# Attention with V as the stationary operand: split values and split, turned probabilities in half sequences, outputs scaled at the end, and half of the preparation on GpSimd

## The chip, the cores and the metric

The kernel runs on one NeuronCore of a Trainium2 chip. The metric is device time of one execution in microseconds (us), as the median of several runs. The page of the profile and every trace row come from one profiled execution. Engines are called as the profile calls them: PE is TensorE (PEld its weight loads), DVE is VectorE, ACT is ScalarE, POOL is GpSimd, SP is SyncE, which here issues most of the transfers.

## What is computed

Two sequences of 512 tokens (plus 16 meta tokens each, so 528 positions per sequence) go through a two-layer encoder: an attention mixer, a feed-forward block, a state-space mixer, a second feed-forward block. The change touches the attention mixer alone. Cut to what matters:

```python
SEQ, N_META = 512, 16                 # two sequences of 528 positions
MLA_HEADS, QK_HEAD_DIM, V_HEAD_DIM = 16, 96, 64

def mla_mixer(u, w_in, q_norm, kv_norm, w_q_up, w_kv_up, q_head_norm, k_head_norm, w_out):
    c_q, c_kv, k_rope = jnp.split(u @ w_in, [384, 640], axis=-1)
    q = (rmsnorm(c_q, q_norm) @ w_q_up).reshape(b, L, 16, 96)
    kv = (rmsnorm(c_kv, kv_norm) @ w_kv_up).reshape(b, L, 16, 128)
    k_nope, v = jnp.split(kv, [64], axis=-1)
    k = jnp.concatenate([k_nope, broadcast(k_rope)], axis=-1)
    q, k = apply_rope(rmsnorm(q, q_head_norm), pos), apply_rope(rmsnorm(k, k_head_norm), pos)
    s = einsum('bqhd,bkhd->bhqk', q, k) / sqrt(96)
    p = softmax(s, axis=-1)
    o = einsum('bhqk,bkhd->bqhd', p, v)
    return o.reshape(b, L, 1024) @ w_out
```

Everything is float32. Most products are made from split operands: a value is written as high + low, both in a rounded type that TensorE multiplies in one pass (`F32R`, fp32r in the rows), and three products (high by high, high by low, low by high) are summed.

## The kernel before

The work is written out by hand as one instruction stream for each engine; semaphores alone order them against each other. Activations lie transposed, features on partitions and the 2 x 528 positions along the free dimension. The program goes through: first norms and the two low-rank projections, attention, the output projection (units `U_OUT`), feed-forward, state-space layer, feed-forward, final norm.

**The attention stage** is a loop over 16 heads `j` and, inside each, 10 turns `n`; turn number `t = 10 j + n`. A turn handles one block of 106 queries (`CW`; five blocks cover a sequence, the last overlaps the one ahead of it by two) against all 528 keys of its sequence. `nxt = j + 1` is the head that is prepared meanwhile. Every engine runs the same double loop, with its own list of what it does in turn `n`:

- PE, `scores(t)` L1489 on: six matmuls of 264 columns (three products of split Q and K by two halves of the keys) into the two banks from `A_SCORE`. There is one such pair of banks, so they wait for the exponentials of turn `t - 1` (`p_full`); only in the last head two pairs alternate (`score_bank`).
- PE, `turn_probs(t - 1)` L1507 on: five transposes that turn the probabilities of the turn before, keys onto partitions (rows of L1513).
- PE, `outputs(t - 2)` L1516 on: five float32 matmuls with the turned probabilities `PT` (106 x 106) stationary and 64 columns of `V` moving (L1528; a float32 matmul leaves two records each).
- PE, then preparation for the next head: `project_q` in turns 0 to 3, `query_norms` (4 and 5), `turn_outputs` of the pair before last (L1479 on), `project_k` (turns 6, 7) and `key_norms` (8, 9) in every even head up to 12, `project_v` (6 to 9) in heads 3, 7 and 11.
- DVE: `take_k` ahead of the turn's maximum where there are keys, then `maximum(t)` (a reduction over the 528 scores L3007, then its scaling L3010), `take_turned(t - 1)` (copy of three transposed blocks, L3018), `invert(t - 1)` (reciprocal of the row sum), then the rest: `scale_keys`, `turn_queries`, `low_q`, `low_k`, `low_weights`, and the small chains `key_factors` (turns 0 and 1 of odd heads) and `query_factors`.
- ACT: `take_q`, `take_k`, `take_turned(t - 1)` (the two other blocks, L2306), `exponentials_of(t)` (L2318, with the sums of the rows), `evict(t - 2)` (outputs times the reciprocal, 106 x 64), then the high halves of Q, K and of weights.
- POOL does nothing from before the first head until the last one, where it splits outputs and weights for the output projection.
- SP loads the weights, saves the key factors of a pair to DRAM and loads them back broadcast over partitions (`save_factors`, `load_factors`).

A pair is two heads (64 + 64 output rows). The outputs of a head lie with queries on partitions in `O`; `turn_outputs` transposes them and ACT copies them to `H` (`take_outputs_of`).

PE does its list strictly in order, so an instruction that waits holds back the next turn's scores. One wait of this kind matters below: bank `A_STAT` takes one set of sums at a time,

```python
def key_norms(p, half):
    pe.wait_ge(k_squared, NSEQ * p + half + 1)
    if half == 0:
        wait_stats("k", p)      # until what stood in A_STAT ahead of it was taken
```

and what stands there ahead of the key sums is the query sums, which the first instruction of `query_factors(nxt, 0)` on DVE takes.

## Time and profile before

| | |
|---|---|
| median of 3 runs | 3041.29 us |
| lowest, highest | 3038.35, 3042.91 us |
| span of the profiled execution | 3038.7 us |
| of that: PE busy | 2967.0 us (98%) |
| DVE, POOL, ACT busy | 1924.1 (63%), 1527.5 (50%), 1176.6 us (39%) |
| granted TensorE clock, mean | 0.992 |

The span runs from the first to the last instruction of the profiled execution; no separate whole time of that execution is given, and the median lies 2.6 us above its span. Busy shares are means over stages that differ; the attention stage with its 160 turns is some 515 us of the span. Matmul records are pipelined and overlap each other, so the distance between two starts on PE tells more than one record's length.

### The profile page before, as it was taken

How to read it: one execution, taken by the hardware profiler on the slowest of the kernel's cores; microseconds unless marked ns; L12 is line 12 of the kernel's file. 1: busy time of each engine (PE TensorE's matmuls, PEld its weight loads, DVE VectorE, ACT ScalarE, POOL GpSimd, SP SyncE). 2: the span in 40 equal slices, each digit the busy share in tenths (PEclk: the TensorE clock that was granted, in tenths of full speed). 3: DMA queues.
4: the chain of work that ended last, by engine and by line, in shares of the span. 5: the costliest groups of instructions: out<-in, count | busy, mean ns of one | idle time of the engine just before them, and what ended most of it. 6: DMA issues, size and time to landing. Idle time of an engine off the chain costs nothing.

```text
span 3038.7 us, 50018 instructions
## 1 busy us (share of the span) xinstructions
PE 2967.0 (98%) x19166; PEld 2684.5 (88%) x19166; DVE 1924.1 (63%) x2960; ACT 1176.6 (39%) x2027; POOL 1527.5 (50%) x997
## 2 busy tenths in 40 slices
PE   8999999999999999999999999999999999999998
PEld 8999999999999999999999988677777788888776
DVE  6677777755534445777788851677778934445666
ACT  4465666641333334553111122232323533334552
POOL 4100000043777777765444444467674577777774
PEclk9999999999999999999999999999999999999998
DMA  3000100021223334442233423333333232235442
GB/s 128 26 30 27 37 26 16 16 100 49 72 95 99 103 100 163 140 144 71 87 117 94 138 90 118 116 119 101 123 94 118 67 107 102 99 103 171 149 130 90
DMA packets 195934, 286.73 MB, mean 94 GB/s; under 512 B 14709, under 2 KB 105077, under 8 KB 195701
## 3 DMA queue, kind: packets, MB, share of 16 engines
q1 hardware_dynamic: 156096, 236.23, 23.8%
q10 hardware_dynamic: 39605, 47.34, 4.7%
q8 instruction: 154, 2.52, 0.3%
q14 instruction: 79, 0.65, 0.1%
HBM read 208.64 MB, written 74.86 MB: 93 GB/s over the span
## 4 chain that ended last, share of the span: by engine, by line
PE 80%; DVE 7%; POOL 5%; issue 4%; DMA 2%; ACT 1%; SPq 1%; DVEq 0%; ACTq 0%; POOLq 0%
PE PS L1272 72%; PE PS L1528 4%; PE PS L1513 2%; DMA Wraw<-in_w 1%; POOL Wlo L1108 1%; POOL Wlo L1168 1%; PE PS L1872 1%; POOL SQ L1213 1%; SPq L911 0%; DVE GD L3627 0%; POOL RMS L1178 0%; POOL Wraw L1126 0%; POOL Wraw L1124 0%; DVE MX L3007 0%; PE PS L2024 0%
## 5 line engine op out<-in xcount | busy, mean ns | idle before, releaser
L1272 PE MATMUL PS<-Uhi,Whi 128*128 128x352 f32 (+2 forms) x2028 | 512.4, 328 | 16.5 <-DVE Ulo L2799 13.8
L1272 PE MATMUL PS<-Uhi,Wlo 128*128 128x352 f32 (+2 forms) x2028 | 507.3, 326 | 0.0
L1272 PE MATMUL PS<-Ulo,Whi 128*128 128x352 f32 (+2 forms) x2028 | 507.0, 326 | 0.0
L1108 POOL TENSOR_TENSOR Wlo<-Wraw,Whi 128x512 fp32r<-128x512 f32 x242 | 329.8, 1366 | 130.4 <-ACT Whi L2442 127.1
L1272 PEld LDWEIGHTS PS<-Uhi,Whi 128*128 128x128 f32 x2028 | 340.9, 189 | 39.4 <-issue 15.9
L1067 POOL TENSOR_TENSOR Whi<-Wraw,const 128x1024 fp32r<-128x1024 f32 x64 | 159.1, 2486 | 418.4 <-PE PS L1272 403.4
L1272 PEld LDWEIGHTS PS<-Ulo,Whi 128*128 128x128 f32 x2028 | 343.5, 189 | 20.3
L1272 PEld LDWEIGHTS PS<-Uhi,Wlo 128*128 128x128 f32 x2028 | 343.4, 189 | 19.5
L2442 ACT ACTIVATE Whi<-Wraw 128x512 fp32r<-128x512 f32 x242 | 151.3, 629 | 330.7 <-POOL Wraw L1126 133.3
L1156 POOL TENSOR_TENSOR Olo<-H,Ohi 128x1056 fp32r<-128x1056 f32 x5 | 12.1, 2444 | 521.8 <-ACT Ohi L2345 521.8
L1272 PE MATMUL PS<-T,Whi 128*128 128x264 f32 (+1 forms) x1328 | 219.1, 288 | 2.1 <-DVE H L3311 1.9
L1272 PEld LDWEIGHTS PS<-T,Whi 128*128 128x128 f32 x1328 | 186.5, 188 | 3.0 <-DVE H L3311 2.4
L3007 DVE TENSOR_REDUCE MX<-PS 106x1 f32<-106x528 f32 x160 | 113.1, 707 | 113.1 <-PE PS L1272 112.4
L3498 DVE SCALAR_TENSOR_TENSOR YC<-XC,cols,YC 128x1052 f32<-128x1052 f32 (+1 forms) x96 | 180.8, 1883 | 3.4
L1070 POOL TENSOR_TENSOR Wlo<-Wraw,Whi 128x1024 fp32r<-128x1024 f32 x64 | 177.0, 2765 | 5.0
L1528 PE MATMUL PS<-V,PT 106*106 106x64 f32 x1600 | 170.0, 254 | 0.5 <-ACT O L2329 0.5
L1528 PEld LDWEIGHTS PS<-V,PT 106*106 106x106 f32 x1600 | 161.8, 173 | 0.6 <-issue 0.6
L2318 ACT ACTIVATE PR<-PS,MX,TOK 106x528 f32<-106x528 f32 x160 | 127.0, 794 | 47.3 <-DVE MX L3010 46.9
L1272 PE MATMUL PS<-T,Wlo 128*128 128x264 f32 (+1 forms) x664 | 135.3, 287 | 0.0
L1272 PE MATMUL PS<-Uhi,OPS 128*128 128x264 f32 (+1 forms) x552 | 126.0, 321 | 1.3 <-DVE H L3311 0.7
L3311 DVE TENSOR_TENSOR H<-H,PS 128x528 f32<-128x528 f32 x140 | 98.1, 700 | 45.3 <-PE PS L1272 43.5
L3330 DVE TENSOR_TENSOR H<-H,PS 128x512 f32<-128x512 f32 x140 | 94.1, 683 | 49.9 <-PE PS L1272 49.9
(431 smaller groups left out, 7114.4 us busy)
## 6 DMA issues: line engine op xcount, KB each, us to landing
Wraw<-in_w SPq DMA_DIRECT2D x192, 256.0 KB, 3.0
Wraw<-in_w SPq DMA_DIRECT2D x91, 512.0 KB, 3.7
Wraw<-in_w SPq DMA_DIRECT2D x168, 128.0 KB, 2.7
xt<-XTT ACTq DMA_DIRECT2D x20, 640.0 KB, 5.7
opd<-HID SPq DMA_DIRECT2D x40, 264.0 KB, 3.4
T<-opd SPq DMA_DIRECT2D x18, 528.0 KB, 4.3
Ulo<-opd SPq DMA_DIRECT2D x17, 528.0 KB, 4.8
Ulo<-opd SPq DMA_DIRECT2D x17, 512.0 KB, 5.5
```

The lines of the kernel that those rows point to most:

```text
L1067: pool.tensor_tensor(Whi[s][:], Wraw[s][:], ones.unsqueeze(1).broadcast_to([P, BLK, P]), ALU.mult)\
L1070: pool.tensor_tensor(Wlo[s][:], Wraw[s][:], Whi[s][:].bitcast(F32), ALU.subtract)\
L1108: pool.tensor_tensor(f.oplo[j % SLOTS], FIRST_S2 if (p, k) == (0, 6) else f.factors[k], f.ophi[j % SLOTS].bitcast(F32), ALU.subtract).then ...
L1272: ins = pe.matmul(out, lhsT, rhs, start=start, stop=stop, skip_group_check=True)
L1513: ins = pe.transpose(PS[0:CW, A_TURN + b // TURN_DVE, b % TURN_DVE * CW:(b % TURN_DVE + 1) * CW], PR[t % 2][:, key_start(b):key_start(b) + ...
L1528: ins = pe.matmul(PS[0:CW, A_OUT, 0:VD], PT[t % 2][:, b, :], V[x // 4 % 2][:, n // KB * KB + b, x // 2 % 2, x % 2 * VD:(x % 2 + 1) * VD], ...
L2318: act.activation(PR[t % 2][:].rearrange("p (h n) -> p h n", h=2), PS[0:CW, score_bank(t):score_bank(t) + 2, 0:QHALF], ACT.Exp, bias=MX[:, ...
L2442: act.activation(f.ophi[j % SLOTS], FIRST_S2 if (p, k) == (0, 6) else f.factors[k], ACT.Copy)\
L3007: step(vec.tensor_reduce(MX[:, t % RING:t % RING + 1], PS[0:CW, score_bank(t):score_bank(t) + 2, 0:QHALF], AX_XY, ALU.max))
L3311: vec.tensor_tensor(h, h, f.down_bank(k, x), ALU.add).then_inc(f.added.sem, 1)
L3330: vec.tensor_tensor(h, h, f.down_bank(k, x), ALU.add).then_inc(f.added.sem, 1)
L3498: ins = vec.scalar_tensor_tensor(y_[:, :, to], x[:, :, of], taps[:, tap:tap + 1], y_[:, :, to], ALU.mult, ALU.add)
```

## The change

Everything lies in the attention stage. `outputs` now works on a half sequence: for head `x`, sequence `s` and half `h`, the stationary operand is a block of values `VH` whose 128 columns are the head's 64 values in high and in low form side by side, and 264 columns of turned probabilities move, first their high part (`PTH`), then their low part (`PTLa`, `PTLb`). The 64 output rows from the high and the 64 from the low values are added afterwards, by ACT (`other_half`) and DVE (`add_outputs`), straight into `H`. There are 4 such steps in a head in place of 10, in the turns that `PV_TURNS` names (11 is turn 1 of the next head). The row sums are kept in `TOK`, inverted once per pair, saved to DRAM and loaded back spread over partitions, and POOL multiplies `H` by them; the last pair is scaled on DVE out of PSUM. `turn_queries`, `scale_keys`, `low_q`, `low_k` and `low_weights`, and the high half of K for odd heads, move to POOL.

```diff
+PV_TURNS = {4: (0, 0), 6: (0, 1), 9: (1, 0), 11: (1, 1)}
...
-        def outputs(t):
...
-            for b in range(KB):
-                ins = pe.matmul(PS[0:CW, A_OUT, 0:VD], PT[t % 2][:, b, :],
-                                V[x // 4 % 2][:, n // KB * KB + b, x // 2 % 2, x % 2 * VD:(x % 2 + 1) * VD],
-                                start=(b == 0), stop=(b == KB - 1), skip_group_check=True)
+        def outputs(x, s, h):
+
+            pe.wait_ge(pt_high, 2 * last_block(x, s, h) + 2)
+            pe.wait_ge(pt_low, 2 * last_block(x, s, h) + 2)
+            pe.wait_ge(v_lo, x + 1)
+            if (x, s, h) != (0, 0, 0):
+                pe.wait_ge(o_evicted, half_number(x, s, h))
+            of = slice(h * QHALF, (h + 1) * QHALF)
             for b in range(KB):
+                low = PTL[b // TURN_FIRST][:, b % TURN_FIRST, of]
+                for i, probs in enumerate((PTH[:, b, of], low)):
+                    ins = mm(PS[:, A_OUT, 0:QHALF], VH[x % 2][:, s * KB + b, :], probs,
+                             start=(b == 0 and i == 0), stop=(b == KB - 1 and i == 1))
...
# ACT, one turn
                 if t >= 1:
-                    take_turned(t - 1)
-                if t >= 0:
-                    exponentials_of(t)
-                if t >= 2:
-                    evict(t - 2)
+                    high_turned(t - 1)
+                exponentials_of(t)
+                if half_at_turn(t, 1):
+                    other_half(*half_at_turn(t, 1))
+                if j and j % 4 == 0 and n == 1:
+                    high_values(j)
                 if nxt < HEADS:
-                    if n == 5:
+                    if n == 3 and nxt % 4:
+                        high_values(nxt)
+                    if n == 6:
                         high_q(nxt)
-                    if n == (1 if nxt % 2 else 6):
+                    if n == 7 and nxt % 2 == 0:
                         high_k(nxt)
...
# DVE, one turn
-                if t >= 0:
-                    maximum(t)
+                maximum(t)
                 if t >= 1:
-                    take_turned(t - 1)
-                    invert(t - 1)
+                    low_turned(t - 1)
+                if half_at_turn(t, 1):
+                    add_outputs(*half_at_turn(t, 1))
+                if j and j % 2 == 0 and n == 1:
+                    invert(j // 2 - 1)
                 if nxt < HEADS:
                     if nxt % 2 == 0 and n < 2:
                         key_factors(nxt // 2, n)
-                    if n == (0 if nxt % 2 else 5):
-                        scale_keys(nxt)
-                    if n == 4:
-                        turn_queries(nxt)
-                    if n == (7 if nxt % 2 else 6):
-                        low_q(nxt)
-                    if n == (2 if nxt % 2 else 7):
-                        low_k(nxt)
-                    if n in ((6, 9) if nxt % 2 else (8, 9)):
+                    if n in (8, 9):
                         query_factors(nxt, n == 9)
...
+        def low_turned(t):
...
+            for b, (k0, k1) in enumerate(((0, TURN_FIRST), (TURN_FIRST, KB))):
+                vec.wait_ge(pt_high, 2 * t + b + 1)
+                vec.tensor_tensor(PTL[b][:, :, at],
+                                  PS[0:CW, A_TURN + b, 0:(k1 - k0) * CW].rearrange("p (b q) -> p b q", q=CW)[:, :, dup:],
+                                  PTH[:, k0:k1, at].bitcast(F32), ALU.subtract).then_inc(pt_low, 1)
...
+        def add_outputs(x, s, h):
+
+            own, n = slice(x % 2 * VD, (x % 2 + 1) * VD), half_number(x, s, h)
+            vec.wait_ge(ob_made, n + 1)
...
# POOL, new: one head
+            if nxt % 2:
+                scale_keys(nxt)
+            if j and j % 4 == 0:
+                low_values(j)
+            if nxt % 2:
+                high_k(nxt)
+                low_k(nxt)
+            if nxt % 4:
+                low_values(nxt)
+            if j % 2 and split_unit(j) is not None:
+                low_weights(j)
+            if j >= 4 and j % 2 == 0:
+                scale_outputs(j // 2 - 2)
+            turn_queries(nxt)
+            if j % 2 == 0 and split_unit(j) is not None:
+                low_weights(j)
+            if nxt % 2 == 0:
+                scale_keys(nxt)
+            low_q(nxt)
+            if nxt % 2 == 0:
+                low_k(nxt)
...
# SP, new: per pair
+        def load_sums(p):
+
+            sp.wait_ge(sums_out, 16 * (p + 1))
+            if p:
+                sp.wait_ge(o_scaled, p)
```

Two places of the order matter below. The first is PE in turn 4 of an even head. Before (rows are engine instructions in program order, `KHI,QHI` are scores, `const,PR` the transposes, `V,PT` the outputs, `const,SQ` the query norms):

```order
L1272 MATMUL PS<-KHI,QHI 106x264 [waits p_full]
L1272 MATMUL PS<-KHI,QHI 106x264
L1272 MATMUL PS<-KLO,QHI 106x264 x2
L1272 MATMUL PS<-KHI,QLO 106x264 x2
L1513 MATMUL PS<-const,PR 106x106 [waits pt_scalar,pt_vector,p_full]
L1513 MATMUL PS<-const,PR 106x106 x4
L1528 MATMUL PS<-V,PT 106x64 [waits o_evicted,pt_scalar,pt_vector]
L1528 MATMUL PS<-V,PT 106x64 x4
L1272 MATMUL PS<-const,SQ 106x1 [waits stats_taken,q_squared]
L1272 MATMUL PS<-const,SQ 106x1 x4
```

The same turn in the changed kernel, from the transposes on (`out_pool` is `v_lo` there):

```order
L1666 MATMUL PS<-const,PR 106x106 [waits pt_low,p_full]
L1666 MATMUL PS<-const,PR 106x106 x2
L1666 MATMUL PS<-const,PR 106x106 [waits pt_low]
L1666 MATMUL PS<-const,PR 106x106
L1417 MATMUL PS<-PTH,VH 128x264 [waits out_pool,o_evicted,pt_low,pt_high]
L1417 MATMUL PS<-PTLa,VH 128x264
L1417 MATMUL PS<-PTH,VH 128x264
L1417 MATMUL PS<-PTLa,VH 128x264
```

Five short output matmuls of each turn became ten of 264 columns in turns 1, 4, 6 and 9 (six more like these follow the last row), and none in turns 0, 2, 3, 5, 7 and 8. The second place is DVE in the even heads with a next pair of keys: before, in turn 6, the query factors begin right behind the reciprocal:

```order
L3007 TENSOR_REDUCE MX<-PS 106x1 [waits sc_full]
L3010 TENSOR_SCALAR MX<-MX,TOK 106x1 [waits vec_steps]
L3018 COPY PT<-PS 106x318 [waits ov_full,pt_full]
L3026 RECIPROCAL SINV<-SSUM 106x1 [waits o_evicted,p_full]
L2940 TENSOR_TENSOR TOK<-PS,TOK 106x10 [waits stats_full]
```

Now they begin in turn 8, behind `take_k` (L3054) and the two subtractions of the low probabilities:

```order
L3165 TENSOR_TENSOR H<-PS,OB 64x264 [waits h_half]
L3054 TENSOR_SCALAR KR<-PS,cols 64x528 [waits k_scaled,k_squared]
L3139 TENSOR_REDUCE PS<-PS 106x1 [waits sc_full]
L3144 TENSOR_SCALAR MX<-PS,TOK 106x1 [waits p_full,vec_steps]
L3154 TENSOR_TENSOR PTLa<-PS,PTH 106x3x106 [waits pt_high]
L3154 TENSOR_TENSOR PTLb<-PS,PTH 106x2x106 [waits pt_high]
L3089 TENSOR_TENSOR TOK<-PS,TOK 106x10 [waits stats_full]
```

The last row is the one that frees bank `A_STAT` for the key norms (`h_half` is `ob_made` here); it moved by two turns, into the same turn as the first `key_norms` of PE.

## Rows read from the trace of the kernel before

**Rows 1.** Busy time by engine from the first maximum to head 15's.

```profile
core 0: us, PE busy (x) PEld busy (x) DVE busy (x) ACT busy (x) POOL busy (x), PEclk, DMA share, GB/s
121.90:614.40 492.50, 479.43 (x4532) 474.80 (x4533) 358.56 (x1025) 308.38 (x753) 0.00 (x0) 1.00 0.07 24
```

**Rows 2.** Timeline of turn 7 of head 5 (start us, us, engine, line, op).

```profile
307.81 0.49 PE L1272 MATMUL PS<-KHI,QHI 128*106 128x264 f32 x2
...
308.63 0.62 PE L1513 MATMUL PS<-const,PR 106*106 106x106 f32 x5
308.83 0.71 DVE L3007 TENSOR_REDUCE MX<-PS 106x1 f32<-106x528 f32 x1 [0.37 <-PE PS L1272]
...
309.08 1.06 PE L1528 MATMUL PS<-V,PT 106*106 106x64 f32 x10
...
309.82 0.79 ACT L2318 ACTIVATE PR<-PS,MX,TOK 106x528 f32<-106x528 f32 x1
...
309.98 0.62 PE L1485 MATMUL PS<-const,O 106*128 106x106 f32 x5
...
310.76 0.48 PE L1272 MATMUL PS<-KHI,QHI 128*106 128x264 f32 x2 [0.15 <-ACT PR L2318]
```

**Rows 3.** Timeline, turns 6 to 8 of head 2, which projects keys.

```profile
206.29 0.49 PE L1272 MATMUL PS<-Chi,Whi 128*128 128x264 f32 x2
...
206.50 0.15 DVE L2940 TENSOR_TENSOR TOK<-PS,TOK 106x10 f32<-106x10 f32 x1
...
207.71 0.17 DVE L2828 SCALAR_TENSOR_TENSOR TOK<-TOK 106x10 f32<-106x10 f32 x1
...
207.85 0.41 PE L1272 MATMUL PS<-KHI,QHI 128*106 128x264 f32 x2
...
208.05 0.61 ACT L2256 ACTIVATE SS<-PS 128x528 f32<-128x528 f32 x1 [0.81 <-PE PS L1272]
...
208.75 0.77 DVE L2905 TENSOR_SCALAR KR<-PS,cols 64x528 f32<-64x528 f32 x1 [0.87 <-ACT SS L2256]
...
209.56 0.71 DVE L3007 TENSOR_REDUCE MX<-PS 106x1 f32<-106x528 f32 x1
...
211.48 0.49 PE L1272 MATMUL PS<-KHI,QHI 128*106 128x264 f32 x2
```

**Rows 4.** Timeline of DVE: first maximum of heads 0, 4, 5, 6, 7, 8, 15.

```profile
121.88 0.69 DVE L3007 TENSOR_REDUCE MX<-PS 106x1 f32<-106x528 f32 x1
...
254.18 0.69 DVE L3007 TENSOR_REDUCE MX<-PS 106x1 f32<-106x528 f32 x1
...
286.76 0.71 DVE L3007 TENSOR_REDUCE MX<-PS 106x1 f32<-106x528 f32 x1 [0.34 <-PE PS L1272]
...
317.73 0.71 DVE L3007 TENSOR_REDUCE MX<-PS 106x1 f32<-106x528 f32 x1 [0.23 <-PE PS L1272]
...
351.58 0.71 DVE L3007 TENSOR_REDUCE MX<-PS 106x1 f32<-106x528 f32 x1 [0.33 <-PE PS L1272]
...
386.65 0.69 DVE L3007 TENSOR_REDUCE MX<-PS 106x1 f32<-106x528 f32 x1
...
614.42 0.71 DVE L3007 TENSOR_REDUCE MX<-PS 106x1 f32<-106x528 f32 x1 [0.23 <-PE PS L1272]
```

**Rows 5.** Groups by line and shape, whole span: prices for new and moved instructions.

```profile
L3647 DVE TENSOR_TENSOR SQ<-PS,EXPC 128x512 f32<-128x512 f32 x32 | 22.0, 686 | 3.2 <-PE PS L1272 3.0
...
L2336 ACT ACTIVATE H<-PS 128x424 f32<-128x424 f32 x16 | 8.3, 522 | 2.4 <-PE PS L1485 2.4
...
L1070 POOL TENSOR_TENSOR Wlo<-Wraw,Whi 128x1024 fp32r<-128x1024 f32 x64 | 177.0, 2765 | 5.0
...
L1156 POOL TENSOR_TENSOR Olo<-H,Ohi 128x1056 fp32r<-128x1056 f32 x5 | 12.1, 2444 | 521.8 <-ACT Ohi L2345 521.8
...
L2794 DVE TENSOR_TENSOR SS<-SS,SQ 128x1056 f32<-128x1056 f32 x9 | 15.5, 1722 | 0.6
```

**Rows 6.** Stretches around the two falls of the granted clock, columns as above.

```profile
111.00:114.40 3.40, 3.40 (x35) 3.40 (x35) 3.33 (x5) 2.17 (x2) 0.00 (x0) 1.00 0.51 160
114.50:117.90 3.40, 3.40 (x18) 3.40 (x17) 2.18 (x10) 0.00 (x0) 0.00 (x0) 0.50 0.00 0
...
636.70:640.10 3.40, 2.68 (x25) 2.43 (x25) 0.67 (x3) 1.00 (x4) 2.37 (x2) 1.00 0.18 74
```

More of the change, by code:

```diff
@@ L371, in key_start @@
     return w // KB * L + min(w % KB * CW, L - CW)
-def turned_pair(j):
-    return j // 2 - 1 if j % 4 == 2 or j % 4 == 1 and j > 1 else None
 def prep_orders():
@@ L389, in prep_orders @@
             stats.append(("t", nxt // 2))
+        elif j:
+            stats.append(("s", j // 2 - 1))
         stats.append(("q", nxt))
-        if turned_pair(j) is not None:
-            prep += [("o", turned_pair(j), s) for s in both]
         if nxt % 4 == 0:
@@ L1583, in _ @@
                         query_norms(nxt, n - 4)
-                    o = 4 if nxt % 2 else 6
-                    if turned_pair(j) is not None and o <= n < o + 2:
-                        turn_outputs(turned_pair(j), n - o)
                     if nxt % 4 == 0 and n >= 6:
@@ L2385, in _ @@
         t = HEADS * PER_HEAD
-        take_turned(t - 1)
-        evict(t - 2)
-        evict(t - 1)
-        take_outputs_of(PAIRS - 1, 1)
+        high_turned(t - 1)
+        for h in range(2):
+            other_half(HEADS - 1, 1, h)
         high_out(PAIRS - 1)
```

387 lines of the change are left out of this document (231 added, 156 removed).

## The prediction

> **What bounds the kernel now.** I read the busy shares first, then the attention stage alone, then single turns. From the first maximum to that of head 15, 492.5 us pass, with PE busy for 479.4 of them, the clock at 1.00 and POOL at nothing [rows 1]. That looks like a stage bound by PE, but the timeline of one turn says otherwise. Scores start at 307.81, the maximum at 308.83 (1.02 later), the exponentials at 309.82 (2.01), the next scores at 310.76: 2.95 us, and that last start waited for ACT [rows 2]. There is one pair of score banks, so scores, maximum, its scaling, exponentials and scores again form a **loop of 2.95 us** that no saving on PE shortens. PE's own list takes longer than the loop in some turns only. Its pieces: scores and transposes 1.27 (307.81 to 309.08), outputs 0.90 (309.08 to 309.98) [rows 2], key projection 1.56 for 12 matmuls of 264 columns (206.29 to 207.85) [rows 3], so 0.13 for each. A turn with nothing else is 2.17 on PE and runs at 2.95; with a first query part (10 matmuls, 1.30) it is 3.47, with a second (8, 1.04) 3.2, with a set of norms (10 short records; at the outputs' 0.09 each, 0.90) 3.07.
>
> A third limit sits in the even heads that project keys. In their turn 7, ACT squares the keys from 208.05, DVE copies them from 208.75, and the maximum starts at 209.56, 1.71 after its scores at 207.85 instead of 1.02; the next scores follow at 211.48, 3.63 later [rows 3]. Turn 8 has the same piece.
>
> A head takes 32.6 us (254.18 to 286.76: keys), 31.0 (to 317.73: odd), 33.9 (to 351.58: keys and turned outputs) or 35.1 (to 386.65: values) [rows 4].
>
> **The change, part by part,** as what each turn costs over the loop of 2.95.
>
> Loop. The maximum goes through PSUM and scaling reads it there; copies and sums from PSUM and SBUF differ by little in price, so 0. ACT now puts two copies (318 and 212 columns; from 0.52 for 424 [rows 5], 0.44 and 0.35 are estimates) ahead of the exponentials where it had one. The transposes end about 1.45 into the turn, the first three about 1.28; the two copies can be through by 1.9, and the exponentials start at 2.01. Loop stays 2.95. Bounds: 2.90 to 3.05, and 150 turns hang on it, so 7 us down, 15 up.
>
> Outputs. 1600 records at 0.09 (144 us) go, 640 matmuls at 0.13 (83 us) come, and 80 transposes with their copies go. PE loses about 70 us of work, but not where it decides: turns 0, 2, 3 and 5 fall to the loop, while turns 1, 4, 6 and 9 now hold 1.27 + 1.30 and their preparation. Turn 1: 1.27 + 1.30 + 1.04 = 3.61 (+0.65). Turn 4: 1.27 + 1.30 + 0.90 = 3.47 (+0.5). Turn 6 with keys: 4.13 (+1.2). Turn 9 with key norms: 3.47 (+0.5).
>
> DVE. Low halves replace the copy: 0.48 + 0.37 (1.04 ns a column and 0.15, from 0.69 for 512 [rows 5]), and end about 2.6 into the turn; `add_outputs` waits for ACT's `other_half`, behind the exponentials, and ends near 3.65. That fits ahead of the next maximum at 2.95 + 1.02 = 3.97, but nothing behind it does. In turn 0 of odd heads `key_factors` follows it: seven small steps, 1.4 us (206.50 to 207.88 for such a chain [rows 3]), to 5.0, so the next maximum is 1.0 late (+1.0, and 0.15 in the turn after). `query_factors` in turns 8 and 9 end near 4.05: +0.1 each.
>
> The bank of sums. In heads with keys `query_factors` moved to turn 8, behind `take_k`, maximum and low halves. `take_k` ends at 1.64, the maximum starts at 1.65, its scaling at 2.39, the low halves take 2.5 to 3.3. Only then is bank `A_STAT` free, and PE stands at `key_norms` with the scores of turn 9 behind it: 3.45 + 0.90 = 4.4 against 2.95 (+1.45; before, 3.6). Turn 7 keeps its 3.64 (+0.7).
>
> POOL. A pass over 1056 columns is 2.44 [rows 5]. An odd head has low values 1.5, low weights 2.4, turned queries 2.4, scaled keys 2.5, low queries and low keys 2.4 each; by its order and ACT's `high_k` in turn 7 the low keys end near 29.2 of some 31.7 us: hidden, by 2.5 us. If that cover goes, the next head's first scores wait. A row bears on it: DVE adding two SBUF operands took 1.72 beside other work [rows 5]. The Trainium skill (GPSIMD Engine Reference, section Specifications) says POOL's SBUF interface is shared with VectorE and contends with DVE instructions that have two SBUF inputs. The new large DVE instructions read one operand from PSUM, so by that rule as by my sum POOL keeps 2.44. Transfers of the sums on SP's queue wait for `o_scaled`, some 17 us into an even head; the weight load behind them is needed a head later: 0. Start and end of the stage: POOL's two first low halves end before the first scores; two spreads of the sums take the place of the turned outputs: +1.
>
> The sum without the clock: keys 7 x (29.5 + 5.0) = 241.5; odd 4 x (29.5 + 2.2, with 0.3 for a late `take_q`) = 126.8; values 3 x (29.5 + 1.15 + 0.5 + 1.05 + 0.1 + 2.75) = 105.2; head 14 29.5 + 1.4 = 30.9; together 504.4 against 492.5: **+12**, +13 with the ends.
>
> **The clock.** At 114.5 the granted clock fell from 1.00 to 0.50 (2.4 to 1.2 GHz) and stayed there for 3.4 us, with PE busy for every moment of the 3.4 us ahead: they held 20 one-column matmuls and only at the end wide ones. It fell again at 640.1, behind 3.4 us with 2.68 busy, five transposes and twenty short outputs [rows 6]. In the attention stage it never fell [rows 1]. Now turns 5, 7 (no keys) and 8 hold six score matmuls and five transposes in 2.95 us, turns 4 and 8 end in one-column norms, and nothing streams between. The thinnest stretch (from the norms of turn 4 to turn 6) is thinner than those ahead of either fall. I expect about one fall in each of 15 heads and another in about half. Each costs what PE does in the 3.4 us that follow once more: in turn 6 or 9 (2.6 to 4.1 us of work) 1 to 1.7 us, in a bare turn 0.7, when the scores double. 22 falls by 0.8 are **+18**; bounds 0 and 22 x 1.7 = 37.
>
> Span: 3038.7 + 13 + 18 = 3070. The median lies 2.6 above the span; I say 3071.
>
> The Trainium skill (TensorE: Matmul & The Clock Gate, "Why this matters for your kernels") speaks for a steady clock here: it ties falls in a kernel to gaps in which TensorE has nothing to do for a long stretch. The fall at 114.5 without any gap disagrees; by the page's rule the result would be the first rival's.
>
> **Rivals.**
> 1. *The clock stays at 1.00.* For: dense outputs of 264 columns in four turns of ten, and 482 us without a fall before. Against: the stretch ahead of 114.5. Then 3041.3 + 13 = 3054. Chance 0.2.
> 2. *Faster: PE's saving is realised.* If DVE's chains don't decide, because the small steps slip in ahead of `add_outputs`' wait or finish sooner, turn 8's 1.45 becomes 0.7 (7 x 0.75 = 5 us), the odd heads' 1.15 goes (7 x 1.15 = 8 us), and outputs at 0.11 each instead of 0.13 give 4 x 0.2 x 15 = 12 us in the turns that PE sets. That is 25 less than +13: 3029, with a steady clock. It decides only if key chain and bank wait both go. Against it: program order on DVE is strict in the listing, and 1.4 us for a chain is a measured row. Chance 0.1.
> 3. *POOL is late.* If each of its passes takes 2.77 for 1024 columns, as the mean of a row says [rows 5], six passes add 2.0 us and eat the 2.5; at 20% more every second head waits some 2 us: 8 x 2 = 16 on top, 3087. Chance 0.07.
>
> My forecast, falls and waits as summed, has 0.63.
>
> **How the numbers follow.** A measurement of this kernel tells a difference of about 0.2% (6 us) from none. The forecast and rival 3 are slower. Of rival 1, 3054 with 8 us of doubt on the loop and the matmul price, 0.13 is slower, 0.05 within, 0.02 faster; of rival 2, 0.07 faster, 0.03 within. Faster 0.09, same 0.08, slower 0.83. The range reaches down to the first rival less half of its doubt, 3045, and up to 3095: 3071 with 37 in place of 18 for the clock and a few us of the loop.
>
> **What would show it.** Right: maxima 2.95 apart in turns 2, 3 and 5; 4.4 between those scores of turns 8 and 9 of key heads, with PE idle for DVE's first query factor; a clock near 0.9 over the stage in stretches of 3.4 us; PE busy share lower; heads of 34 to 36 us (keys). Wrong: a clock of 1.00 through the stage (then near 3054); a loop under 2.90, or key heads under 33 us (then rival 2); rows in which the first scores of a head wait for POOL's low keys (rival 3); or a difference outside of 120 to 645 us, where the instruction streams are the same.

## The result and the profile after

| | before | after |
|---|---|---|
| median, lowest to highest (us) | 3040.7, 3038.4 to 3042.9 | 3126.1, 3123.1 to 3132.7 |
| ratio, 95% interval | | 1.028, 1.027 to 1.030 |
| span of the profiled execution | 3038.7 | 3122.3 |
| granted TensorE clock, mean | 0.992 | 0.972 |

The change makes the kernel 85 us slower. I forecast slower with a chance of 0.83, but by 30 us, and the range ended at 3095: the sign was right, the size was not. The spans differ by 83.6 us. Where they lie, from the first maxima of heads: head 0 to head 15 takes 565.8 us in place of 492.5 (+73.3), head 15 23.7 in place of 20.4 (+3.3), the end of the stage up to the output projection 10.5 in place of 6.3 (+4.2), everything else +2.8. So the stage of 15 heads is the place. One of the four executions of run 4 below took 4278.9 us at a granted clock of 0.62; its time is left out there.

Busy time from the first maximum to that of head 15 in the changed kernel, and two stretches in it and behind it (for the columns and the row of before see [rows 1]):

```profile
core 0: us, PE busy (x) PEld busy (x) DVE busy (x) ACT busy (x) POOL busy (x), PEclk, DMA share, GB/s
121.60:687.40 565.80, 478.97 (x3580) 454.98 (x3581) 369.20 (x1020) 338.64 (x792) 222.26 (x116) 0.90 0.09 28
697.20:700.60 3.40, 3.27 (x16) 3.28 (x17) 1.49 (x4) 3.39 (x7) 3.39 (x2) 0.51 0.02 5
711.00:721.50 10.50, 8.73 (x78) 7.93 (x78) 4.36 (x12) 3.29 (x10) 1.78 (x1) 0.68 0.18 55
```

PE's busy time is what it was, 479 us, but part of that is now work at half clock: 0.90 is a fifth of the stage at 1.2 GHz. 87 us of the stage are idle time of PE; before it was 13. DVE has 11 us more, though large passes left it.

Here is what holds DVE up. The timeline of DVE, then of POOL, at the end of head 1 (start us, us):

```profile
188.27 0.37 DVE L3154 TENSOR_TENSOR PTLb<-PS,PTH 106x212 fp32r<-106x212 f32 x1
188.55 0.31 DVE L2973 TENSOR_TENSOR TOK<-TOK 106x10 f32<-106x10 f32 x1
188.90 0.52 DVE L2975 SCALAR_TENSOR_TENSOR TOK<-TOK 106x10 f32<-106x10 f32 x1
189.45 0.17 DVE L2977 SCALAR_TENSOR_TENSOR TOK<-TOK 106x10 f32<-106x10 f32 x1
189.66 1.80 DVE L2973 TENSOR_TENSOR TOK<-TOK 106x10 f32<-106x10 f32 x1
191.50 0.17 DVE L2975 SCALAR_TENSOR_TENSOR TOK<-TOK 106x10 f32<-106x10 f32 x1
191.70 2.27 DVE L2977 SCALAR_TENSOR_TENSOR TOK<-TOK 106x10 f32<-106x10 f32 x1
194.00 0.17 DVE L3098 SCALAR_TENSOR_TENSOR TOK<-TOK 106x10 f32<-106x10 f32 x1
194.09 0.71 DVE L3139 TENSOR_REDUCE PS<-PS 106x1 f32<-106x528 f32 x1
```

```profile
187.00 1.84 POOL L1180 TENSOR_TENSOR KSC<-KR,KFB 128x848 f32<-128x848 f32 x1 [1.44 <-PE PS L1417]
188.80 0.60 POOL L1182 TENSOR_TENSOR KSC<-KR,KFB 128x208 f32<-128x208 f32 x1
189.47 1.97 POOL L1188 TENSOR_TENSOR KHI<-KSC,const 128x1056 fp32r<-128x1056 f32 x1
191.52 2.42 POOL L1193 TENSOR_TENSOR KLO<-KSC,KHI 128x1056 fp32r<-128x1056 f32 x1
```

Add start and length. A step of 106x10 takes 0.17 us when nothing holds it. Four of these end later: at 188.86, 189.42, 191.46 and 193.97. POOL's four passes end at 188.84, 189.40, 191.44 and 193.94, each 0.02 or 0.03 earlier. The steps behind the second and the third of them begin in the gap before POOL's next pass and take 0.17; behind the fourth POOL has no pass. So the seven steps from 188.55 on, 1.4 us otherwise, last to 194.17, and the first maximum of head 2 stands behind them: turn 9 of head 1 takes 7.15 us, where a turn of the loop is 2.95. Over the stage the groups of the query chain on DVE read (behind the bar: busy us, mean ns, idle us before):

```profile
L2977 DVE SCALAR_TENSOR_TENSOR TOK<-TOK 106x10 f32<-106x10 f32 (+1 forms) x66 | 20.8, 315 | 2.3
L2975 DVE SCALAR_TENSOR_TENSOR TOK<-TOK 106x10 f32<-106x10 f32 (+1 forms) x66 | 18.5, 280 | 2.3
L2973 DVE TENSOR_TENSOR TOK<-TOK 106x10 f32<-106x10 f32 (+1 forms) x66 | 16.1, 244 | 1.5
L3091 DVE TENSOR_SCALAR TOK<-TOK 106x10 f32<-106x10 f32 x15 | 7.3, 485 | 0.5
L3098 DVE SCALAR_TENSOR_TENSOR TOK<-TOK 106x10 f32<-106x10 f32 x15 | 2.6, 170 | 0.5
```

Before, the same groups took 166 to 173 ns. At that price these five groups would be 39 us and are 65: 26 us more, in chains that a maximum waits behind. (The first three hold 21 steps of the key chains each, "+1 forms".) It is the query chains of odd and values heads, in turns 8 and 9, when POOL makes keys, low queries and low halves of weights. The key chains (106x20, in turns 0 and 1 of these heads) kept their 0.18 us: POOL has no pass then. In turns 8 and 9 of heads with keys it has none either, so their query chains are not held.

The second thing is the clock. Stretches of 3.4 us in turns 7 to 9 of head 2, which projects keys, and in turns 6 to 8 of head 1, which does not:

```profile
219.40:222.80 3.40, 2.85 (x23) 2.46 (x22) 2.65 (x6) 2.63 (x7) 1.51 (x1) 1.00 0.00 0
222.80:226.20 3.40, 1.13 (x13) 0.95 (x11) 3.02 (x10) 2.27 (x6) 0.00 (x0) 1.00 0.00 0
226.20:229.60 3.40, 3.40 (x19) 3.39 (x19) 1.25 (x5) 0.23 (x1) 0.00 (x0) 0.50 0.00 0
229.60:233.00 3.40, 3.40 (x19) 3.40 (x19) 2.07 (x11) 1.35 (x4) 0.00 (x0) 0.50 0.01 2
```

```profile
175.00:178.40 3.40, 2.69 (x22) 2.47 (x21) 2.43 (x7) 2.38 (x7) 3.40 (x3) 1.00 0.00 0
178.40:181.80 3.40, 1.65 (x12) 1.44 (x13) 1.62 (x4) 2.94 (x8) 2.43 (x2) 1.00 0.64 179
181.80:185.20 3.40, 2.19 (x12) 1.83 (x11) 2.42 (x7) 2.71 (x6) 2.31 (x2) 0.50 0.34 135
```

In head 2 PE works for 1.13 us of the stretch ahead of the fall, and the trace says why: it waits 2.3 us for the first query factor on DVE, which frees bank `A_STAT` (the row of the waits follows). At half clock turn 9, full of outputs and key norms, then takes 6.2 us. In head 1 PE waits for nothing longer than 1.5 us ahead of the fall, which stands behind one bare turn: turn 7 has scores and transposes from 178.63 to 180.08 and nothing until 181.60.

```profile
PE PS L1417 <- DVE TOK L3089: 15.9, 7, 2.3
PE PS L1417 <- POOL Wlo L1209: 0.8, 2, 0.5
```

The second row: PE waited for POOL 0.8 us in all (columns: us in total, times, longest). POOL itself is not late.

### The profile page after: what moved, and what is told of

Read it like the earlier page. It is cut to its first block, busy times and chain, and to the rows that moved or that the text cites. A ratio compares the mean times of both kernels' runs of the same rounds, so it can differ in the third digit from the quotient of the medians.

```text
span 3122.3 us, 47932 instructions
## 1 busy us (share of the span) xinstructions
PE 2971.6 (95%) x18181; PEld 2669.4 (85%) x18181; DVE 1940.6 (62%) x2962; ACT 1209.6 (39%) x2067; POOL 1753.5 (56%) x1115
## 4 chain that ended last, share of the span: by engine, by line
PE 71%; DVE 11%; issue 6%; POOL 6%; ACT 3%; DMA 2%; SPq 1%; POOLq 0%; ACTq 0%; DVEq 0%
PE PS L1417 69%; DVE PS L3139 2%; DMA Wraw<-in_w 1%; PE PS L1666 1%; POOL Wlo L1253 1%; ACT PR L2480 1%; POOL Wlo L1313 1%; DVE MX L3144 1%; PE PS L2026 1%; POOL SQ L1358 1%; SPq L972 0%; DVE TOK L2977 0%; DVE GD L3767 0%; POOL RMS L1323 0%; POOL Wraw L1271 0%
## 5 line engine op out<-in xcount | busy, mean ns | idle before, releaser
L3139 DVE TENSOR_REDUCE PS<-PS 106x1 f32<-106x528 f32 x160 | 114.3, 714 | 111.9 <-PE PS L1417 110.8
L2468 ACT ACTIVATE PTH<-PS 106x318 fp32r<-106x318 f32 (+1 forms) x320 | 107.6, 387 | 166.3 <-PE PS L1666 166.2
L1417 PE MATMUL PS<-KHI,QHI 128*106 128x264 f32 x320 | 80.8, 336 | 61.2 <-ACT PR L2480 59.7
L1199 POOL TENSOR_TENSOR VH<-V,VH 106x640 fp32r<-106x640 f32 x16 | 25.0, 1566 | 201.0 <-ACT VH L2448 201.0
```

What stands on the lines that cost most here:

```text
L1417: ins = pe.matmul(out, lhsT, rhs, start=start, stop=stop, skip_group_check=True)
L2468: act.activation(PTH[:, k0:k1, key_start(n) + dup:key_start(n) + CW], PS[0:CW, A_TURN + b, 0:(k1 - k0) * CW].rearrange("p (b q) -> p b q", ...
L3139: step(vec.tensor_reduce(most, PS[0:CW, score_bank(t):score_bank(t) + 2, 0:QHALF], AX_XY, ALU.max))
```

## The experiments

"Heads with keys" project keys for the next pair (0, 2, 4 to 12), "odd" heads are 1, 5, 9, 13, "values" heads 3, 7, 11. The ratio is to the kernel before, run beside it on the same chip, with its 95% interval. The runs were made on four chips, on which the medians of the kernel before were 3041.3 to 3043.5 us, so differences of 2 us between runs say nothing.

**1. Query factors of heads with keys in turns 6 and 7.**

```diff
+            if p:
+                pe.wait_ge(qs_ready, 2 * p)
...
-                    if n in (8, 9):
-                        query_factors(nxt, n == 9)
+                    early = nxt % 2 and nxt + 1 < HEADS
+                    if n in ((6, 7) if early else (8, 9)):
+                        query_factors(nxt, n == (7 if early else 9))
```

The wait at the top is new in PE's `key_norms`: they now begin only when the whole chain is done.

> The changed kernel with the query factors of heads that project keys in turns 6 and 7 instead of 8 and 9, so that bank A_STAT is free before key_norms of turn 8; nothing else. Theory 'port' (DVE's small factor steps, which read SBUF only, are held until the POOL pass that runs beside them ends, 0.17 us becoming up to 2.3): the chain of these heads moves away from POOL's last passes, so the 15.9 us that PE waited for the first query factor go and some of the 27 us of stretched steps too: 15 to 25 us faster than the changed kernel's 3126, i.e. 3101 to 3111. Theory 'bank' (only the wait for the bank matters): 10 to 16 us, 3110 to 3116, steps of turns 6 and 7 still stretched. Theory 'clock' (falls of the granted clock carry the excess): under 8 us, 3118 to 3126.

Measured: 3127.1 us, 1.028 (1.027 to 1.030): no gain, a miss of the first two theories. PE's wait for the bank is gone, but the chain stands in turn 7, which grows from 3.8 to 4.9 us, turn 8 is 3.6, and turn 9 is 6.2 us, at half clock, in five of the seven heads. A whole chain moved is a new delay; this did not tell what the wait alone costs (run 9 does).

**2. The same, and no factor step reads two operands from SBUF.** One operand of each stands in spare columns of bank `A_STAT`; the wait of run 1 also keeps PE off this bank:

```diff
+        def held(i, n=1):
+            ap = PS[0:CW, A_STAT, 384 + i * 2 * KW:384 + i * 2 * KW + n * KW]
...
-            rsqrt_rounds(y, tok(K_V), tok(K_TMP), 2)
+            rounds_held(held(4), tok(K_V), tok(K_TMP), 2)
```

> As e4_early_factors, and every step of the query and key factors reads one operand from PSUM and at most one from SBUF (same number of steps). Theory 'port': the steps stay at 0.15 to 0.18 us beside POOL, none over 0.3; another 15 to 25 us faster than e4. Theory 'bank' or 'clock': within 4 us of e4. If PSUM operands do not free the steps from POOL, they stay at up to 2.3 us.

Measured: 3103.1 us, 1.020 (1.018 to 1.022), 24 less than run 1. The groups of the chain in this kernel:

```profile
L3081 DVE SCALAR_TENSOR_TENSOR PS<-TOK,PS 106x10 f32<-106x10 f32 (+1 forms) x68 | 12.0, 177 | 2.3
L3080 DVE SCALAR_TENSOR_TENSOR TOK<-TOK,PS 106x10 f32<-106x10 f32 (+1 forms) x67 | 11.3, 169 | 2.3
L3079 DVE TENSOR_TENSOR TOK<-PS,TOK 106x10 f32<-106x10 f32 (+1 forms) x67 | 11.2, 167 | 1.6
```

Same steps, same places, same POOL passes beside them, and 167 to 177 ns. Odd heads 5 and 9 fall from 38.0 and 37.4 us to 33.1.

**3. Idle matmuls in the bare turns** (6 or 12 products of 264 columns into a free bank, turns 5, 7 and 8; results not used).

```diff
+                for _ in range(6 if n == 5 or keys else 12):
+                    pe.matmul(PS[0:CW, A_PREP, 0:QHALF], Chi[:, 0, 0:CW], Chi[:, 1, 0:QHALF],
+                              start=True, stop=True, skip_group_check=True)
```

> The changed kernel with idle matmuls of 264 columns into an unused bank in the turns without outputs (6 in turn 5 and in turn 8 of key heads, 12 in turns 7 and 8 of the other odd heads). They compute nothing that is used. Theory 'clock': the granted clock over the attention stage rises from 0.90 to 0.97 or more and the time falls by 15 to 35 us against 3126, to 3091 to 3111. Theories 'port' and 'bank': the clock may rise, but the time stays within 8 us of 3126, because the late turns 8 and 9 are not set by PE.

Measured: 3098.4 us, 1.018 (1.016 to 1.019): 28 us less with more work on PE. The clock of the stage rises from 0.90 to 0.96. Heads with keys fall to 34.5 to 34.9 us from head 4 on; odd ones stay at 36.5 to 37.3, with one turn of 7.6 us where DVE's chain is held.

**4. V stationary alone: preparation back on DVE and ACT,** in the turns that it had before the change.

```diff
-            pool.tensor_tensor(QLO[x % 2][:], QS[x % 2], QHI[x % 2][:].bitcast(F32), ALU.subtract).then_inc(q_lo, 1)
+            vec.tensor_tensor(QLO[x % 2][:], QS[x % 2], QHI[x % 2][:].bitcast(F32), ALU.subtract).then_inc(q_lo, 1)
...
+                    if n == (0 if nxt % 2 else 5):
+                        scale_keys(nxt)
+                    if n == 4:
+                        turn_queries(nxt)
+                    if n == (7 if nxt % 2 else 6):
+                        low_q(nxt)
+                    if n == (2 if nxt % 2 else 7):
+                        low_k(nxt)
```

> The changed kernel with the preparation of queries, keys and weights back on DVE and ACT in the turns of the kernel before (query factors too, at 6 and 9 in even heads); POOL keeps only low values and the scaling of outputs. Theory 'port': without POOL passes beside them the factor steps are 0.17 us and no head's last turns stretch, but DVE is longer: 3065 to 3085. Theory 'clock': only what the bank gives, 3100 to 3120. If V as the stationary operand were itself a gain and all loss the move to POOL, this kernel would be at or below the kernel before's 3041.

Measured: 3149.5 us, 1.035 (1.033 to 1.037): another 23 us slower, a miss of all numbers. The first 518.5 of the 594.6 us of its stage:

```profile
121.50:640.00 518.50, 428.87 (x3155) 408.21 (x3155) 380.67 (x960) 302.44 (x698) 34.66 (x19) 0.89 0.09 27
```

POOL has next to nothing, so it holds no chain, but DVE is busy for 380.7 us and its passes, 1.24 to 1.9 us each in the mean, stand between the maxima: heads with keys take 38 to 44 us. Before the change DVE had room for the preparation; with the low halves of the probabilities (126 us for 298 instructions in the changed kernel) it has not. The clock is 0.89, no better than with the move. So the move to POOL cost what POOL holds up and still helped on balance.

**5 to 7. POOL beside the kernel before.** 150 passes of 128x1056 whose result nothing uses, from the first exponentials on; only ACT's last copies ahead of the output projection wait until they are done:

```diff
+        for n in range(150):
+            if n:
+                pool.wait_ge(idle_done, n)
+            pool.tensor_tensor(H[:, KD - 1, :], Chi[:, 0, :].bitcast(F32), Clo[:, 0, :].bitcast(F32), ALU.mult).then_inc(idle_done, 1)
```

In the second kernel the pass is

```diff
+            pool.tensor_scalar(H[:, KD - 1, :], Chi[:, 0, :].bitcast(F32), 1.5, None, ALU.mult).then_inc(idle_done, 1)
```

and in the third it runs over `piece = slice(n % 4 * 264, n % 4 * 264 + 264)`, 600 times.

> The kernel before with 150 multiplications of 128x1056 on POOL beside attention, one after the other from the first exponentials on (both operands in SBUF, the result is thrown away), over heads 0 to about 10; nothing else is changed, and no engine waits for them before the last pair's outputs. Theory 'port': DVE's steps of 106x10 that read two SBUF operands go from 0.17 us each to means above 0.3 with single ones of 1.5 us or more that end with a pass; chains of seven then take 3 us or more, their turns grow, and DVE's large additions and products of two SBUF operands beside a pass as well: 15 to 60 us slower, 3057 to 3100. Rival 'port for chains alone': 5 to 15 us. Rival 'the steps were long by their place in the changed kernel, not by POOL': 3043 and no step above 0.2. The clock stays near 1.00 where the turns stay under 3.7.

> The kernel before with 150 passes of 128x1056 on POOL as in the run that was 157 us slower, but each a multiplication by a constant (TENSOR_SCALAR, one operand in SBUF) in place of a product of two. Theory 'two operands on POOL make the hold': DVE's small steps stay at 0.17 to 0.3 us and the time within 20 us of the kernel before, under 3063. Rival 'any pass of POOL holds them': the same stretched steps (means of 0.4 to 1.7 us), 3120 to 3200, less where a pass is shorter.

> The kernel before with the same 158400 columns of two-operand products on POOL, cut into 600 passes of 264 columns. Theory 'a step is held until the pass that runs has ended': the longest step falls from over 2 us to about 0.8 (0.61 a pass and 0.17), the means of the factor steps to about 0.5, and the loss to a third or a half of 157: 3090 to 3120. Rival 'held as long as POOL has work': steps of over 1.5 us remain and the time is near 3200.

| POOL beside the kernel before | median, ratio (interval) |
|---|---|
| product of two SBUF operands, 150 passes of 1056 | 3200.6, 1.052 (1.050 to 1.054) |
| product with a constant, 150 passes of 1056 | 3048.9, 1.0025 (1.0014 to 1.0035) |
| product of two, 600 passes of 264 | 3117.8, 1.025 (1.023 to 1.027) |

In the first kernel the passes end at about 530 us, in head 7, long before ACT asks: work that nobody waits for costs 157 us, all of it in heads 0 to 7. A key chain of DVE in it follows; POOL's row shows five passes from 164.86 on, and the second to fourth of them end at 169.78, 172.31 and 174.86:

```profile
168.74 1.07 DVE L2936 TENSOR_TENSOR TOK<-TOK 106x20 f32<-106x20 f32 x1
169.84 0.18 DVE L2824 TENSOR_SCALAR TOK<-TOK 106x20 int32<-106x20 int32 x1
170.06 2.29 DVE L2827 TENSOR_SCALAR TOK<-TOK 106x20 int32<-106x20 int32 x1
172.38 0.18 DVE L2834 TENSOR_TENSOR TOK<-TOK 106x20 f32<-106x20 f32 x1
172.60 2.30 DVE L2836 SCALAR_TENSOR_TENSOR TOK<-TOK 106x20 f32<-106x20 f32 x1
174.94 0.18 DVE L2838 SCALAR_TENSOR_TENSOR TOK<-TOK 106x20 f32<-106x20 f32 x1
```

```profile
164.86 12.53 POOL L1159 TENSOR_TENSOR H<-Chi,Clo 128x1056 f32<-128x1056 f32 x5
```

A step that begins beside a pass ends 0.03 or 0.04 us behind it; the next begins in the gap and takes 0.18, so about every second one waits a whole pass. All 60 steps with two SBUF operands that begin during a pass of this run end behind it. With passes of 264 columns (0.74 us each where DVE leaves them alone) the second part of the same chain reads:

```profile
160.43 0.16 DVE L2835 TENSOR_TENSOR TOK<-TOK 106x20 f32<-106x20 f32 x1
160.63 0.73 DVE L2837 SCALAR_TENSOR_TENSOR TOK<-TOK 106x20 f32<-106x20 f32 x1
161.40 0.18 DVE L2839 SCALAR_TENSOR_TENSOR TOK<-TOK 106x20 f32<-106x20 f32 x1
161.61 0.63 DVE L2835 TENSOR_TENSOR TOK<-TOK 106x20 f32<-106x20 f32 x1
```

A step is held until the pass that runs has ended, no longer. The 76 us of this kernel are not all of that kind: its last piece ends at 684 us, in head 15, and ACT waits 26.8 us for it there. Head 15 takes 53.8 us in place of 20.4, and the 15 heads ahead of it 533.5 in place of 492.5. So the short passes cost 41 us over 15 heads by their hold, the long ones 162 in heads 0 to 7.

With one operand on POOL, though its passes are longer (2.92 us), the loss is 8 us, and the three groups of 57 steps are at 174 to 266 ns; the pass, and two of them:

```profile
L1159 POOL TENSOR_SCALAR H<-Chi 128x1056 f32<-128x1056 f32 x146 | 425.8, 2916 | 40.1 <-ACT PR L2324 28.1
...
L2834 DVE TENSOR_TENSOR TOK<-TOK 106x10 f32<-106x10 f32 (+1 forms) x57 | 15.2, 266 | 1.3
...
L2838 DVE SCALAR_TENSOR_TENSOR TOK<-TOK 106x10 f32<-106x10 f32 (+1 forms) x57 | 9.9, 174 | 1.9
```

The hold is not gone there, it is shorter. Four smaller groups have means of 0.35 to 0.73 us. Two passes, a step near the end of the first and one at the start of the second:

```profile
216.32 5.85 POOL L1159 TENSOR_SCALAR H<-Chi 128x1056 f32<-128x1056 f32 x2
219.13 0.17 DVE L2838 SCALAR_TENSOR_TENSOR TOK<-TOK 106x10 f32<-106x10 f32 x1
219.34 1.03 DVE L2959 SCALAR_TENSOR_TENSOR TOK<-TOK 106x10 f32<-106x10 f32 x1
```

Of the 200 DVE steps with two SBUF operands that begin during such a pass, the 23 that begin in its first 0.9 us are all held, and all end 1.09 to 1.12 us after the pass began; the 177 that begin later are not held. TENSOR_SCALAR steps of DVE are held in the same first part (10 of 13), and those that begin 1.8 to 2.7 us into the pass (all 11) to its end. So a small step of DVE that reads and writes SBUF is held by either kind of pass: by a product of two SBUF operands to its end, by a product with a constant for the first 1.1 of 2.9 us. Why it ends there the runs don't tell.

**8. Two cures together, and a third.** The first kernel has the idle matmuls, and the PSUM chains but for the query chain of heads with keys, which stays where and as it was. The second is the changed kernel with the key factors ahead of `add_outputs` in turn 0 of odd heads, alone. The third has all of it. The edit of the second:

```diff
+                if nxt < HEADS and nxt % 2 == 0 and n == 0:
+                    key_factors(nxt // 2, 0)
                 if half_at_turn(t, 1):
                     add_outputs(*half_at_turn(t, 1))
```

> The changed kernel with both cures at once: idle 264-column matmuls in the bare turns, and the key and query chains on DVE written so that no step reads two operands from SBUF (one stands in PSUM), but for the query chain of heads with keys, which keeps its place and its form. Theory 'clock and port, separate': the fillers alone gave 28 us and the PSUM chains 24, of which the heads with keys had next to nothing; so heads with keys stay at 34.5 to 35 us, odd heads fall from 37.0 to 33 or less, values heads from 37.1 to under 36, together 4 x 4 + 3 x 1.5 = 20 less than with fillers alone: 3078, bounds 3070 and 3085. Rival 'one cause': the long chains are what leaves PE thin, so that with one cured the other is worth under 5: 3093 to 3098. No POOL pass is touched; the rest over the kernel before (about 35 us) is loop, outputs in turns 1, 4, 6, the bank wait and the chain in turn 0.

> The changed kernel with one thing moved on DVE: in turn 0 of odd heads the key factors stand ahead of the addition of the outputs, which waits for ACT's other half, instead of behind it. Theory 'order on DVE': turn 0 of these heads falls from 4.16 to 3.0 to 3.2 us, 7 or 8 us in all, unless the addition then ends late and holds PE's outputs in turn 1 (it ends near 4.5 of turn 0, and PE wants the bank at about 1.3 of turn 1: little). 3118 to 3121. Rival 'POOL holds the steps wherever they stand': the chain also stretches ahead of the addition and turn 0 stays above 3.8: 3124 to 3128.

> The first kernel of this call (idle matmuls and PSUM chains) with the key factors ahead of the addition too. Theory: turn 0 of odd heads at 3.0 to 3.2, 5 to 7 us less than the first kernel, about 3072. Rival 'no cover': the same time, the loss reappears in turn 1. If all three cures together leave it at 3065 to 3075, the change is a loss of 25 to 35 us by its outputs (turns 1, 4, 6), the bank wait and the end of the stage, and no order of DVE's work saves it.

Measured: 3074.7 (1.010, 1.008 to 1.012), 3122.2 (1.026, 1.025 to 1.028) and 3074.6 us (1.011, 1.009 to 1.013). Idle matmuls and PSUM chains add up: 24 less than with idle matmuls alone. Turn 0 falls from 4.16 to 3.4, not to 3.1, and turn 1 grows from 2.95 to 3.4: more than half of it is given back. By itself it gives 4 us, with intervals that overlap those of the changed kernel, and nothing that can be measured on top of the others. "No cover" was nearly right.

**9. One step moved: the bank of sums freed in turn 6.** On the third kernel of 8, and alone on the changed kernel:

```diff
+                    if n == 6 and nxt % 2 and nxt + 1 < HEADS:
+                        query_factors(nxt, -1)          # its first step only, 0.16 us
                     if n in (8, 9):
                         query_factors(nxt, n == 9)
```

> The changed kernel with idle matmuls, PSUM chains and the key factors ahead of the addition (3074.6), and one thing more: in heads with keys the first step of the query factors, which frees the bank of sums, stands in turn 6 by itself; the rest of the chain stays in turns 8 and 9. Theory 'bank wait': turn 8 of these heads falls from 3.87 to about 3.5 and turn 9 stays at 3.3 where the clock holds: 7 x 0.4 = 3 us, 3070 to 3072. Rival: take_k in turn 8 sets it as before the change, nothing gained, 3074. Either way it stays above 3055: the rest over the kernel before is PE's list in turns 1, 4 and 6 and the end of the stage.

> The changed kernel with only one thing moved: in heads with keys the step that frees the bank of sums stands in turn 6. Theory 'the bank wait starts the falls': turn 8 of these heads goes from 4.4 to 5.4 down to about 3.1, turn 9 to 3.3, 7 heads by 2 to 3 us: 3104 to 3112. Rival 'small by itself', since the held query chain (turns 8 and 9) and the falls of turns 5 to 8 stay: under 8 us, 3118 to 3126.

Measured: 3055.3 us (1.0043, 1.0028 to 1.0057) and 3113.2 us (1.025, 1.022 to 1.027). One step of 0.16 us is worth 19 us on top of the other cures (17 when each kernel is set against its own run of the kernel before) and 13 alone; I had expected 3 for the first and 14 to 22, or under 8, for the second. The stage in the first of them, and the stretch in head 2 that answers to the one of 1.13 us busy (six idle matmuls are in it):

```profile
121.25:616.09 494.84, 459.41 (x3802) 436.00 (x3803) 339.92 (x1020) 339.47 (x792) 222.88 (x116) 1.00 0.10 32
```

```profile
211.40:214.80 3.40, 2.85 (x26) 2.58 (x25) 3.17 (x11) 1.88 (x5) 0.00 (x0) 1.00 0.00 0
```

Turn 8 is 3.03 us and turn 9 3.29 in every head with keys, and the clock falls once in the stage, at 611.0 in head 14. What the gain is made of: in the profile of the third kernel of 8, turn 8 of these heads was 3.86 to 4.14, so the wait was worth 6.4 us over seven heads and not 3; turn 9 was 3.29 in three of them and 4.6 to 4.8 in four, where the clock fell behind the wait, another 5.6. Alone on the changed kernel, turn 8 gives 12 us, part of which it had run at half clock, and turn 9 nothing: it still takes up to 5.9 at half clock. So in that profile the wait and the fall behind it weigh about the same, and the fall went only where the idle matmuls stood. It was the fastest of four executions (3065.6 us; the others 3074.6 to 3079.5), so at the median the share of the clock is probably larger, which no trace shows.

**10. The best version with one cure taken out, and one more placed.** Without the idle matmuls; with the chains in SBUF as in the change; with the outputs of the first sequence in turns 5 and 7 in place of 4 and 6:

```diff
-PV_TURNS = {4: (0, 0), 6: (0, 1), 9: (1, 0), 11: (1, 1)}
+PV_TURNS = {5: (0, 0), 7: (0, 1), 9: (1, 0), 11: (1, 1)}
```

> The best version so far (3055: idle matmuls, PSUM chains, key factors ahead of the addition, bank of sums freed in turn 6) without the idle matmuls. Theory 'waits make the falls': with no wait over 1 us left on PE the clock holds by itself in most heads, 0.97 or more over the stage, and the time is 3055 to 3065. Rival 'thin turns make the falls': bare turns of 2.17 us of work in 2.95 are enough for them, clock near 0.92, some 15 to 20 falls at 1 us or more each: 3072 to 3085.

> The best version so far with the key and query chains as in the changed kernel, with two operands in SBUF. Theory 'POOL's hold costs what the maxima are late': odd heads 31.0 back to 36 or 37 (turns 8 and 9), values heads 34.9 to 36.5, heads with keys little: 4 x 5.5 + 3 x 1.5 = 27, 3078 to 3086. Rival 'only with a falling clock': under 10 us, 3055 to 3065.

> The best version so far with the outputs of the first sequence in turns 5 and 7 in place of 4 and 6 (idle matmuls then in turns 6 and 8). Theory: turn 5 takes ten matmuls within its 2.95, so turn 4 falls from 3.37 to 2.97 in 15 heads, 6 us; in heads with keys turn 6 falls by 1.1 and turn 7 grows by 0.9 to 1.3: 3047 to 3050, still 6 to 9 above the kernel before. Rival: turn 7's keys, copies and outputs together start a fall or a wait: 3055 to 3062.

Measured: 3078.8 (1.012, 1.010 to 1.015), 3090.0 (1.016, 1.015 to 1.018) and 3078.7 us (1.013, 1.010 to 1.015). The stages of the first two:

```profile
121.57:642.29 520.72, 461.26 (x3579) 440.51 (x3580) 341.08 (x1020) 338.20 (x792) 222.42 (x116) 0.93 0.10 30
```

```profile
121.56:650.79 529.23, 471.83 (x3802) 448.55 (x3803) 368.87 (x1019) 339.06 (x792) 222.81 (x116) 0.96 0.09 29
```

Without idle matmuls the clock falls again, in bare turns without a long wait, as the rival of the expectation has it: 24 us. With the held chains 35 us where I expected 27: turn 8 of odd heads is 7.6 in place of 3.0, and falls of the clock stand behind such late maxima (0.96 over the stage in place of 1.00). The third missed: turn 4 does fall to 3.14 in most heads, but turn 5 of heads with keys goes to between 3.3 and 6.0 and turn 8 to 3.9, and the clock of the stage is 0.96 again. The idle matmuls had moved too, to turns 6 and 8, so the turns ahead of turn 5 are the thin ones now.

No version beat the kernel before; the best is 0.4% slower. It was not tried to keep PE fed at the end of the stage, where that version runs at half clock from the last maximum (638.25) to the output projection (650.77): 12.5 us in place of 6.3.

## Why the prediction was wrong in size

Taken one after the other, the 85 us divide so: freeing the bank in turn 6 gives 13 (3126.1 to 3113.2); idle matmuls, with the key factors moved, 23 (to 3090.0); chains that POOL cannot hold 35 (to 3055.3); 14 remain over the kernel before. In another order the shares differ, as the clock joins them: the bank gives 17 to 19 when it comes last, and PSUM chains gave 24 on other kernels (runs 2 and 8).

**Loop: right.** Maxima 2.93 to 2.99 apart in turns 2, 3 and 5 where the clock holds.

**Outputs: near.** Turn 1 is 3.4 us (3.61 forecast), turn 4 3.37 (3.47): a matmul of the outputs is 0.12 from start to start at full clock (140.13 to 140.98 for seven), not 0.13. Turn 6 with keys is 4.6, and 5.3 in heads 4, 8 and 12 (4.13). Turn 0 of odd heads is 4.16 (3.95).

**POOL: the step that failed.** I asked only whether DVE would slow POOL ("The new large DVE instructions read one operand from PSUM, so by that rule as by my sum POOL keeps 2.44"). POOL kept 2.45 and was never waited for, as forecast. I did not ask what POOL does to DVE, and priced the chains as "`query_factors` in turns 8 and 9 end near 4.05: +0.1 each", from a kernel in which POOL did nothing in this stage. They end up to 4 us later, in odd and values heads. The row on which I stood, an addition of 1.72 us "beside other work", had the effect in it: 1.72 is a mean of additions of 1.25 us with no POOL pass ahead of them and of single ones of 3.3 to 3.4 that began while a POOL pass of 3.3 us ran (one at 24.36). I used it for POOL's side alone. This term was put at 0.1 us a turn; it measured 35 us in all, falls of the clock that it starts included.

The Trainium skill (GPSIMD Engine Reference, section Specifications) names DVE instructions in a 2-port perf mode or with two SBUF inputs as the ones that contend with POOL. The runs agree for the second kind, and one operand from PSUM frees them (167 to 177 ns). A DVE TENSOR_SCALAR with one SBUF input is held as well (L3091, 485 ns, up to 1.23 us; L2827 above, 2.29 us); it may be of the first kind, which no trace here shows. I had the rule in hand and asked only whether POOL would wait.

**Bank of sums: right in mechanism and wait, near in price.** Forecast +1.45 in turn 8 of heads with keys, 10 us in all; the wait is there, 15.9 us in 7 heads, and freeing the bank alone gives 13. I forecast clock falls by what bare turns look like and did not join them to this wait, which leaves PE 1.13 us of work in 3.4; that part shows when the bank is freed last.

**Clock: right in kind, too small.** The clock is 0.90 over the stage, as I wrote for "near 0.9", but I priced 22 falls at 0.8 (18 us). A fifth of 565.8 us at 1.2 GHz is 113 us, or 33 stretches of 3.4 us, half more than I counted, and several lie in the turns with most work: turn 9 of heads with keys takes 4.1 to 6.2 us, and 3.29 in the best version; turn 6 up to 5.8, and 4.6 or 5.3 there. Idle matmuls give 23 to 28 us back. The first rival, a steady clock, fell, and with it the rule that ties falls to long gaps (the Trainium skill, TensorE: Matmul & The Clock Gate, "Why this matters for your kernels"): in the version without idle matmuls PE's longest waits are 1.5 us and the clock is 0.93.

**End of the stage:** +1 forecast; +3.3 in head 15 and +4.2 behind it measured, with the clock at 0.68 in the latter.

**Rivals.** Faster by PE's saving: even with both waits gone the stage is 494.8 us against 492.5, since the loop sets half of the turns. POOL late, 3087: its time was nearer than mine, by a mechanism that isn't there.

**Range:** its lower end doesn't follow from its own words: 3054 less half of 8 is 3050, not 3045. Nothing hangs on it, as the time lies above the upper end.

## What to carry to other kernels

Before work is moved to POOL, look for chains of small SBUF steps on DVE beside it: each can be held for as long as a POOL pass with two SBUF operands lasts, and if a maximum that PE needs stands behind the chain, its turn grows by passes, not by steps. Such chains can read one operand from PSUM (24 to 35 us here), or POOL be given passes with one operand or short ones, which were tried beside the kernel before alone. Where PE has slack, a stall of 2 us is priced with the clock: look whether what comes next is heavy, and free a shared bank by its first small step at the earliest turn instead of moving the whole chain.
